# One of two weight sums per quad in a streaming encoder's MLP: made by GpSimd instead of by a DMA

## The reference

```python
x = x + jnp.concatenate([ret_out, conv_out], axis=-1) @ w_out
h2 = rms_norm(x, ln2_w)
x = x + jnp.square(jax.nn.relu(h2 @ w_up)) @ w_down
```

## Time and profile before

| | us |
|---|---|
| median of 3 runs | 1404.87 (1402.94 to 1405.62) |
| the profiled execution, its own time | 1403.99 |
| its span in the profile | 1401.98 |
| TensorE matmuls busy | 1381.7 (99%) |
| VectorE busy | 897.2 (64%) |
| ScalarE busy | 594.9 (42%) |
| GpSimd busy | 166.0 (12%) |
| TensorE's granted clock over the span | 0.998 of full speed |

### The profile page before, as it was taken

One profiled execution on the slowest core, in us unless ns is written; L12 is line 12 of the kernel. 1 busy time (PEld: TensorE's weight loads), 2 busy tenths in 40 slices (PEclk: granted clock), 3 DMA queues, 4 the chain that ended last, 5 costly groups with the idle time before them and its releaser, 6 DMA issues.

```text
span 1402.0 us, 21312 instructions
## 1 busy us (share of the span) xinstructions
PE 1381.7 (99%) x7750; PEld 1242.3 (89%) x7750; DVE 897.2 (64%) x1104; ACT 594.9 (42%) x712; POOL 166.0 (12%) x185
## 2 busy tenths in 40 slices
PE   8999999999999999999999999999999999999997
PEld 6888999889889899899878889998898998998986
DVE  6336515269976867868861474262788678688586
ACT  5211222157636446446533012231584464464563
POOL 2343200010000000000033431000100000000001
PEclk9999999999999999999999999999999999999999
DMA  7424212126454645455142242113345454544623
GB/s 274 136 76 122 83 50 73 55 105 156 88 153 121 150 98 149 140 116 159 31 134 102 91 121 68 61 62 120 76 129 142 110 158 124 121 121 121 151 61 105
DMA packets 91614, 158.18 MB, mean 113 GB/s; under 512 B 3892, under 2 KB 21428, under 8 KB 91512
## 3 DMA queue, kind: packets, MB, share of 16 engines
q1 hardware_dynamic: 74472, 123.18, 26.1%
q0 software_dynamic: 16896, 33.56, 14.1%
q10 hardware_dynamic: 144, 0.07, 0.0%
HBM read 149.38 MB, written 7.41 MB: 112 GB/s over the span
## 4 chain that ended last, share of the span: by engine, by line
PE 95%; DVE 1%; issue 1%; ACT 1%; DMA 0%; POOL 0%; SPq 0%; DVEq 0%; POOLq 0%; ACTq 0%
PE pair L776 27%; PE pair L615 23%; PE pair L832 21%; PE pair L625 12%; PE pair L845 6%; PE pair L665 2%; PE pair L703 1%; PE pair L710 1%; PE pair L684 1%; PE pair L688 1%; PE pair L693 1%; DMA w_raw<-in_w_in 0%; PE pair L696 0%; DVE ring L1738 0%; DVE x L1784 0%
## 5 line engine op out<-in xcount | busy, mean ns | idle before, releaser
L776 PE MATMUL pair<-mlp_in_hi,ring 128*128 128x320 f32 x1728 | 381.5, 309 | 0.0
L1104 ACT ACTIVATE ring<-raws 128x1024 fp32r<-128x1024 f32 x220 | 230.9, 1058 | 250.0 <-PE pair L832 129.8
L1738 DVE TENSOR_TENSOR ring<-raws,ring 128x1024 fp32r<-128x1024 f32 x220 | 267.1, 1221 | 103.0 <-ACT ring L1104 101.6
L832 PE MATMUL pair<-ring,a_ring 128*128 128x512 f32 x1344 | 312.1, 390 | 0.0
L832 PEld LDWEIGHTS pair<-ring,a_ring 128*128 128x128 f32 x1344 | 251.9, 188 | 52.5
L776 PEld LDWEIGHTS pair<-mlp_in_hi,ring 128*128 128x128 f32 x1728 | 289.1, 188 | 0.2
L776 PE MATMUL pair<-mlp_in_lo,ring 128*128 128x320 f32 x864 | 266.8, 309 | 0.0
L776 PEld LDWEIGHTS pair<-mlp_in_lo,ring 128*128 128x128 f32 x864 | 162.1, 188 | 0.2
L625 PE MATMUL pair<-norm_hi,ring 128*128 128x320 f32 x512 | 114.5, 310 | 0.0
L615 PE MATMUL pair<-ring,norm_hi 128*128 128x512 f32 x320 | 100.5, 395 | 2.7 <-DVE norm_lo L1502 2.6
L615 PE MATMUL pair<-pair_a,norm_hi 128*128 128x512 f32 x320 | 100.9, 397 | 0.0
(11 more groups left out here) (161 smaller groups left out, 1943.9 us busy)
## 6 DMA issues: line engine op xcount, KB each, us to landing
raws<-in_w_mlp_up SPq DMA_DIRECT2D x32, 1024.0 KB, 5.5
raws<-in_w_mlp_down SPq DMA_DIRECT2D x32, 1024.0 KB, 5.1
w_raw<-in_w_in SPq DMA_DIRECT2D x27, 1024.0 KB, 6.0
raws<-in_w_mlp_up POOLq DMA_DIRECT2D x16, 1024.0 KB, 9.0
raws<-in_w_mlp_down POOLq DMA_DIRECT2D x16, 1024.0 KB, 8.8
w_raw<-in_w_out SPq DMA_DIRECT2D x8, 1024.0 KB, 5.1
past_state<-in_state_ret SPq DMA_DIRECT2D x8, 512.0 KB, 4.4
out_ret_s<-past_state SPq DMA_DIRECT2D x8, 512.0 KB, 4.9
```

Of the source, the lines that this page charges most:

```text
L776: mm = pe.matmul(out[:, n, 0:HALF], item_half(item, h, a)[:, k, n * P:(n + 1) * P], mlp_in[i][c][:, k], start=(i in (B11, B21, SUM_1112, B ...
L832: mm = pe.matmul(out[:], a_item[:, a, 2 * h + k, pair * P:(pair + 1) * P], item_half(item, h, c)[:, k], start=(i in (B11, B21, SUM_1112) a ...
L1104: nc.scalar.activation(item_half(item, h, 0), raw_half(quad, RAW_OF[i], h), ACT.Copy).then_inc(half_hi.sem, 1)
L1738: nc.vector.tensor_tensor(item_half(item, h, 1), raw_half(quad, RAW_OF[i], h), f(item_half(item, h, 0)), ALU.subtract).then_inc(half_lo.se ...
```

## The change

The sum 12 + 22 is no longer made by a DMA. GpSimd reads both quarters where they lie in `raws` and adds in place, in two halves of 128 x 1024 elements. It waits for the same signal as before, and also for the load of quarter 22. ScalarE's split of SUM_1222 then waits for its own half alone. The second sum (21 onto 11) stays a DMA, behind the adds in GpSimd's queue.

```diff
-        onto_12 = Signal("onto_12", 16 * QUADS)
+        onto_12 = Signal("onto_12", 2 * QUADS)
...
                     elif i == SUM_1222:
-                        act.wait_ge(onto_12.sem, onto_12.at(layer, 16 * (quad + 1)))
+                        act.wait_ge(onto_12.sem, onto_12.at(layer, 2 * quad + h + 1))
...
                 for quad in range(QUADS):
                     pool.wait_ge(weights_summed.sem, weights_summed.at(layer, sums_to(quad, SUM_1112, 1)))
-                    add_onto(quad, "12", "22", onto_12)
+                    slot = slot_of(quad, "22")
+                    pool.wait_ge(slot_in[slot].sem, slot_in[slot].at(layer, 16 * (quad + 1)))
+                    for h in range(2):
+                        out = raw_half(quad, "12", h)
+                        nc.gpsimd.tensor_tensor(out, out, raw_half(quad, "22", h), ALU.add).then_inc(onto_12.sem, 1)
                     pool.wait_ge(half_lo.sem, half_lo.at(layer, 2 * (quad * PRODUCTS + SUM_111222) + 2))
                     add_onto(quad, "11", "21", onto_11)
```

## The result

| | before | after |
|---|---|---|
| median of 4 runs each on one chip, us | 1403.95 (1402.94 to 1405.62) | 1414.87 (1413.06 to 1415.59) |
| profiled execution, us (its span) | 1403.99 (1401.98) | 1415.09 (1413.1) |

The changed kernel is slower: the ratio is 1.0074, with an interval from 1.0059 to 1.0089. The two medians are 10.9 us apart; by the interval the difference lies between 8.3 and 12.5. (The ratio here and in the table of the experiments is not exactly that of the two medians; it can differ from it by a few hundredths of a per cent.) The forecast was 1417.0, 2.1 us too high.

The account below looks back on a forecast made before the run. TensorE, with matmuls busy 99% of the span, was taken as the bound. Down quads 10.6 plus first up quads 1.6 made 12.2 us, forecasting 1417.0 from the 1404.87 median; range 1403 to 1422.

Parts of the forecast that it names:

- Nothing gained by the DMAs that go: Sixteen summing DMAs, their issue on GpSimd and 16 x 1 MB of traffic removed: worth 0.
- The exclusion holds in both directions: GpSimd's adds block VectorE's two-SBUF-input instructions too: 0 to 4.7 us per quad, the whole taken; chance 0.57.
- VectorE hardly gives way: Rival in the down stage: ready VectorE instructions pass waiting adds, only one add gets in; no change, 1405, chance 0.25.
- isn't held at all: Rival: the adds don't hold VectorE at all; no change, 1405, chance 0.10.
- Size of an add: A 128x1024 add on GpSimd, start to start: 2.33 us, between 1.85 and 2.53.
- Down quads: Eight quads: TensorE's sample product waits 1.33 us for sample_mid_lo; 10.6 us in sum (3.0 to 13.8).
- No second wait in the stage: Later in the down stage nothing more: VectorE 2 us late, TensorE 1.3 late, tightest room 1.1 us.
- First up quads: Each layer's first up quad: TensorE waits about 0.8 us for a ring half, twice, 1.6 us.
- The other six up quads: Ring half delayed to at most 511, needed by TensorE at 515.0: cost 0.
- GpSimd's own queue: The other summing DMA, 21 onto 11, stands behind 5 us of adds where GpSimd waits 15.34 us: 0.
- The base: Median of the unchanged kernel's runs to which the forecast cost was added: 1404.87 us.

Follow-up runs that it names:

- e8: e6 with the DMA again in each layer's first up quad, so 28 adds stay; 1405.11 us against 1404.78 of before.
- e5: Before with both DMAs kept, plus 8 unused GpSimd memsets per quad that read nothing, the DMA issued behind them; 1404.11 us against 1403.55 of before.
- e6: After, but in down quads GpSimd's second add waits for VectorE's second difference of hidden parts; 1405.51 us against 1404.74 of before.
- e3: After, with VectorE making the sample's low part ahead of the difference in down quads; 1412.26 us against 1404.74 of before.
- e2: After with the adds in the 8 up quads only, the down quads keeping the DMA; 1405.96 us against 1404.74 of before.
- e1: After with the adds in the 8 down quads only, the up quads keeping the DMA; 1412.87 us against 1404.74 of before.
- e7: e3 with VectorE's SUM_111222 additions into x also moved ahead of a weight half; 1406.09 us against 1404.78 of before.
- e4: Before with both DMAs kept, plus 4 unused GpSimd adds per quad reading the same tiles, the DMA issued behind them; 1411.69 us against 1403.55 of before.

## Why the prediction was right

- **Nothing gained by the DMAs that go** (0): right. e8 has 14 fewer and is 0.3 us above before; e5 issues them 5 us later at no cost.
- **The exclusion holds in both directions.** This was the step that the trace of before did not show, with 0 and 4.7 us as its ends, and the upper end was taken. It was argued, not read from a row, and carried the chance of 0.57. After shows it: two instructions of VectorE stretched in each down quad. The rivals at 1405, that VectorE hardly gives way or isn't held at all, are refuted by the 3.43 us rows.
- **Size of an add.** Alone it takes 2.40 us (e6: 2.40 and 2.43), a little over the 2.33 taken. What it costs VectorE is less: 3.35 us from start to start (557.30 - 553.95) where 1.14 is usual, so 2.2 us. The difference is the overlap in which one engine begins while the other ends.
- **Down quads**: place, number and cause right, size too large. On the clock of before the sample's low part ended at 562.48 - 2.62 = 559.86 where 560.09 was forecast. The cost of each was 1.06 us, not 1.33, in sum 8.5 instead of 10.6. The step that was off is the add: both together took 4.4 us from VectorE, not 4.66. The room was right: 559.86 is 1.10 us behind the load at 558.76.
- **No second wait in the stage**: right for after, and e3 shows how narrowly. The prediction had 2 us of lateness against 1.1 of room, covered by a TensorE that is itself 1.3 late. With the first wait taken away the second appears, at 0.8.
- **First up quads**: 0.55 instead of 0.8 us each, and two steps ahead of where it was placed. VectorE is 1.7 us late (1.9 forecast). The prediction says that VectorE has no gap there, but the earlier trace rows show one of 0.21 us, which takes up a part. The first thing that TensorE lacks is the hidden sum that follows the in_diff subtraction, which the prediction did not look at, not the ring half for the load at 328.14. That half alone would have cost 0.5 us, and the earlier wait hides it. The sign and the count of two were right; the tile was wrong, and that the two sizes are so alike is luck.
- **The other six up quads**: 0, right; the tightest ring half had 4 us of room by the prediction's bound of 511 against 515.0, more by the 508.1 measured, and the period of e2 is that of before.
- **GpSimd's own queue**: 0, right; the DMA that stays lands 9.1 us after its issue, and no new wait of TensorE for a DMA stands in the table.

In sum the repeated waits are 9.8 us where 12.2 were forecast, 2.4 too much. The base, 1404.87, came out 0.9 lower, as 1403.95. Both together would put the forecast 3.2 us too high. It is only 2.1 too high, since the medians are 1.1 us further apart than the waits explain, and that part is luck. The single edits fit the same sum: 8 x 1.06 = 8.5 for e1 (8.1 measured), 2 x 0.55 for e2, e6 and e7 (1.2, 0.8 and 1.3), 8 x 0.82 + 1.1 = 7.7 for e3 (7.5), 7.3 for e4 (8.1).

## What to carry to other kernels

In these runs an addition on GpSimd that reads SBUF was paid by VectorE as well, wherever VectorE worked on two SBUF tiles: 2.2 of its 2.40 us. So count nearly its whole length once more in VectorE's queue, and lay it beside instructions that read PSUM. What this costs in the end is not the length but the lateness less the room of each tile that the bound engine needs; list all such needs in the stage, because the earliest hides the others, as e3 found out. Here, with TensorE 99% busy, neither a freed DMA nor less traffic gave anything back: the best versions (e6, e7, e8) only come back to the time of before.

## What the runs showed beside this

**The two engines take turns.** In the stages read here none goes twice while the other has an instruction of the excluded kind waiting: add, a_ring, add, ring in after, and in e4 a_ring, add, ring, add, diff, add, sample_mid_lo, add, ring. Which of them is first is decided by hundredths of a microsecond (553.89 against 553.95 in after, 553.97 against 553.94 in e4), and then the other stands for the whole instruction.

**TensorE's clock at the turn between the layers.** After loses 1.5 us there that the prediction doesn't have. The chain of after and of before at this place:

```profile
715.34 4.61 PE pair L615 x12
```

```profile
710.68 3.03 PE pair L615 x12
```

The same 12 matmuls take 4.61 instead of 3.03 us. In the stretches (busy us of PE, PEld, DVE, ACT, POOL, granted clock, DMA share, GB/s), after and before:

```profile
717.00:719.00 2.00, 2.00 (x7) 1.54 (x6) 1.27 (x3) 0.00 (x0) 0.65 (x1) 0.50 1.05 389
```

```profile
712.00:714.00 2.00, 2.00 (x13) 1.65 (x12) 1.61 (x3) 0.00 (x0) 0.31 (x1) 1.00 1.06 390
```

The granted clock is 0.50 there, the 1.2 GHz level, against 1.00, the 2.4 GHz level. Just ahead TensorE waits for norm_lo, 1.95 us in after and 1.69 in before. In the ten profiles the five in which it idles longest there (after, e1, e2, e6, e8: 1.95 to 3.21 us) take 4.6 us for these matmuls, the other five (before, e3, e4, e5, e7: 1.2 to 1.7) take 3.0 to 3.1. The adds alone don't decide it: e3, e4 and e7 have them and stay at 3.0.

I count these 1.5 us as scatter of the single execution, not as a part of the change. The other runs speak for it. The profiles of e1, e2, e6 and e8 have the slow matmuls too, yet the medians of these kernels lie within 0.4 us of what the waits alone give (8.1 for 8.5, 1.2 for 1.1, 0.8 for 1.1, 0.3 for 0), and the runs of before alone, over all comparisons, spread from 1402.75 to 1408.03 us. Where the remaining 1.1 us between the 9.8 of the account and the 10.9 of the medians go was not shown; with four runs each and an interval from 8.3 to 12.5, 9.8 lies inside.
